# Repeated decay rows of a state-space mixer: from matmuls with ones to loads from DRAM, all four heads of a group at a time

## The reference

```
xbc = silu(causal_conv4(xbc));  xs, bm, cm = split(xbc)      # 4 groups of 4 heads, 64 wide; state 128
dt = softplus(dt_raw + dt_bias);  a_cum = cumsum(dt * -exp(a_log))       # per head and token
lmat = exp(where(l >= s, a_cum[l] - a_cum[s], -inf))
y_diag = (cm . bm) * lmat @ (xs * dt)
y_off = (cm . state_before) * exp(a_cum)
y = y_diag + y_off + d_skip * xs;  g = y * silu(z);  out = g * rsqrt(mean(g*g)) * norm_w
```

## Time and profile before

| what | value |
|---|---|
| median of 3 runs | 1801.18 us (1800.72 to 1802.22) |
| the profiled execution's own time | 1802.67 us |
| its span, first to last instruction | 1800.9 us |
| PE busy | 1749.4 us, 97% of the span |
| chain that ended last | PE 89%, DVE 7%, ACT 2% |
| DVE, ACT, POOL busy | 739.6, 636.9, 711.3 us |
| mean granted clock of TensorE | 0.99 |

### The profile page before, as it was taken

The page is one execution under the profiler, slowest core; times in us unless marked ns, Lnnn a source line. Parts: engine busy times, 40 slices in busy tenths (PEclk is TensorE's granted clock), DMA queues, the critical chain, the costliest instruction groups (busy, mean ns, idle before and its releaser), DMA issues.

```text
span 1800.9 us, 21799 instructions
## 1 busy us (share of the span) xinstructions
PE 1749.4 (97%) x7922; PEld 1413.6 (78%) x7922; DVE 739.6 (41%) x1230; ACT 636.9 (35%) x855; POOL 711.3 (39%) x303
## 2 busy tenths in 40 slices
PE   7999999999999999999899999999989999999996
PEld 6888888888888888888778777777748787888884
DVE  4222322222111324113653555537599544365226
ACT  5333332333222224213632545353352344352112
POOL 3433334334444444442344334333314333325445
PEclk9999999999999999999899999999999999999998
DMA  5432232232322334332433222122203222217322
GB/s 202 127 90 88 88 94 88 88 100 82 100 93 95 102 92 142 120 117 70 170 92 113 69 72 94 68 82 74 81 25 102 73 72 79 82 59 267 119 82 94
DMA packets 51260, 177.68 MB, mean 99 GB/s; under 512 B 5352, under 2 KB 5608, under 8 KB 50032
## 3 DMA queue, kind: packets, MB, share of 16 engines
q1 hardware_dynamic: 41472, 152.13, 26.9%
q10 hardware_dynamic: 9712, 24.48, 3.8%
HBM read 168.18 MB, written 8.40 MB: 98 GB/s over the span
## 4 chain that ended last, share of the span: by engine, by line
PE 89%; DVE 7%; ACT 2%; issue 1%; POOL 1%; DMA 0%; ACTq 0%; SPq 0%; DVEq 0%; POOLq 0%
PE bank L332 88%; PE bank L336 2%; DVE bias L1566 1%; DVE feats L1089 1%; DVE top L1562 1%; DVE bias L1089 1%; POOL w_lo L310 1%; ACT w_hi L718 0%; DMA raw<-in_stream 0%; DVE padded L1342 0%; ACT probsT L1018 0%; ACT bank L914 0%; ACT L1007 0%; DVE stats L1238 0%; DVE planes_lo L1285 0%
## 5 line engine op out<-in xcount | busy, mean ns | idle before, releaser
L310 POOL TENSOR_TENSOR w_lo<-raw,w_hi 128x1024 fp32r<-128x1024 f32 x280 | 685.7, 2453 | 1073.1 <-ACT w_hi L718 1073.1
L332 PE MATMUL bank<-planes_hi,w_hi 128*128 128x512 f32 (+1 forms) x1792 | 709.5, 396 | 19.1 <-DVE w_lo L1151 9.5
L332 PE MATMUL bank<-planes_lo,w_hi 128*128 128x512 f32 (+1 forms) x1792 | 694.7, 388 | 0.0
L332 PE MATMUL bank<-planes_hi,w_lo 128*128 128x512 f32 (+1 forms) x1776 | 687.7, 387 | 0.0
L718 ACT ACTIVATE w_hi<-raw 128x1024 fp32r<-128x1024 f32 x280 | 296.9, 1060 | 911.1 <-PE bank L332 876.9
L332 PEld LDWEIGHTS bank<-planes_hi,w_hi 128*128 128x128 f32 x1792 | 339.7, 190 | 104.0 <-issue 30.6
L332 PEld LDWEIGHTS bank<-planes_lo,w_hi 128*128 128x128 f32 x1792 | 340.1, 190 | 70.5 <-issue 4.8
L332 PEld LDWEIGHTS bank<-planes_hi,w_lo 128*128 128x128 f32 x1776 | 336.2, 189 | 68.1
L332 PE MATMUL bank<-w_hi,planes_hi 128*128 128x512 f32 x512 | 200.4, 391 | 0.0
L332 PE MATMUL bank<-w_hi,planes_lo 128*128 128x512 f32 x512 | 199.3, 389 | 0.0
L332 PE MATMUL bank<-w_lo,planes_hi 128*128 128x512 f32 x512 | 199.2, 389 | 0.0
(11 more groups left out here) (244 smaller groups left out, 1272.2 us busy)
## 6 DMA issues: line engine op xcount, KB each, us to landing
raw<-in_stream SPq DMA_DIRECT2D x282, 512.0 KB, 3.6
h_rows<-feats ACTq DMA_DIRECT2D x4, 1024.0 KB, 7.0
feats<-in_x_t SPq DMA_DIRECT2D x3, 1024.0 KB, 10.7
rope_q<-cum_dram ACTq DMA_DIRECT2D x8, 256.0 KB, 3.1
bias<-in_x_rows ACTq DMA_DIRECT2D x2, 1024.0 KB, 6.1
probs<-in_x_rows ACTq DMA_DIRECT2D x2, 1024.0 KB, 7.9
bias<-h_rows ACTq DMA_DIRECT2D x2, 1024.0 KB, 7.6
probs<-h_rows ACTq DMA_DIRECT2D x2, 1024.0 KB, 8.7
```

The source lines that it names most:

```text
L310: nc.gpsimd.tensor_sub(w_lo[:, s, :], raw[:, s, :], w_hi[:, s, :].bitcast(fp32)).then_inc(lo_ready, 1)
L332: return nc.tensor.matmul(o, a, b, start=start, stop=stop)
```

## The change

The rows are no longer repeated by PE. In the preparation ACT stores `cumT` and its exponential `R[2]` to a DRAM tensor `decay_dram`. For each group SP loads four rows of each, every row repeated over 128 partitions (256 KB a load): L rows into four `LB` tiles as soon as the heads of the group before are done, E rows into four `EB` tiles one weight unit later. These loads stand in SP's list between those of the weights. The tiles lie in buffers free at that time, for which the load of `rope_q` moves behind the stage and `R` from `probs` to `bias`.

All 16 spreads and 16 `pick_row` go, and so do the exponentials from PSUM. `segments` becomes a `tensor_scalar` in place in SBUF (subtract, minimum with zero); the mask is now a multiplication of the scores by zeros and ones, once per group, in PSUM. DVE makes the segments of all four heads in a row between `ssd_carry` and `conv_tile` 1. ACT takes their four exponentials in one go, after tile 1's `Silu`. `operands` 0 and 1 now stand behind `conv_tile` 2, operands 2 and 3 behind `conv_tile` 3; on PE the heads stay where they are.

```diff
+    decay_dram = nc.dram_tensor("decay_dram", [2 * SSD_HEADS, S], fp32, kind="Internal").ap()
...
-        LB = [tmp[:, :], probsT[:, 2, :]]
-        EB = [probsT[:, 3, :], qT[:, :]]
+        LB = [rope_q[:, 0, :], rope_q[:, 1, :], vN[:, 0, :, :].rearrange("p j n -> p (j n)"), gate[:, :]]
+        EB = [probsT[:, 3, :], qT[:, :], kT[:, 0, :], kT[:, 1, :]]
+        SQ = [tmp[:, :], probsT[:, 2, :]]
...
-        MM_STEPS, VEC_STEPS, EXP_STEPS = 14, 17, 10
+        MM_STEPS, VEC_STEPS, EXP_STEPS = 10, 13, 6
...
-            with sp.Fori(2, ROUNDS) as m:
+            def load_next(m, s):
+                sp.wait_ge(lo_ready, 4 * m + s - 7)
+                load(m, s)
+
+            def load_decay(g, of, bufs):
+                for r in range(4):
+                    row = SSD_HEADS * of + 4 * g + r
+                    sp.dma_start(bufs[r], decay_dram[row:row + 1, :].to_broadcast([P, S])).then_inc(decay_loaded[r], 16)
+
+            m0, p0 = tile_at(T_SSD, 6)
+            with sp.Fori(2, m0 + 2) as m:
                 for s in range(4):
-                    sp.wait_ge(lo_ready, 4 * m + s - 7)
-                    load(m, s)
+                    load_next(m, s)
+            for g in range(GROUPS):
+                for u in range(12):
+                    if u == 2 * p0:
+                        if g:
+                            sp.wait_ge(ssd_mm, MM_STEPS * (g - 1) + 9)
+                        else:
+                            sp.wait_ge(decay_kept, 32)
+                        load_decay(g, 0, LB)
+                    load_next(m0 + 2 + 3 * g + u // 4, u % 4)
+                    if u == 2 * p0:
+                        load_decay(g, 1, EB)
+            with sp.Fori(m0 + 2 + 3 * GROUPS, ROUNDS) as m:
+                for s in range(4):
+                    load_next(m, s)
...
-            step(nc.gpsimd.memset(upper[:, :], 0.0))
-
-            select(upper[:, :], ALU.is_ge, -BIG, 0, [[1, P]], -1)
+            step(nc.gpsimd.memset(upper[:, :], 1.0))
+
+            select(upper[:, :], ALU.is_ge, 0.0, 0, [[1, P]], -1)
...
-                srcs = [cumT[:, :]] + [probs[0:SSD_HEADS, k, :] for k in range(4)]
+                srcs = [cumT[:, :]] + [bias[0:SSD_HEADS, k, :] for k in range(4)]
...
-            def ssd_spread(g, r):
-                pe.wait_ge(ssd_vec, VEC_STEPS * g + (4, 6, 10, 13)[r])
-                mm([M, O][r % 2][:, :], ones[0:SSD_HEADS, :], gT[0:SSD_HEADS, :]).then_inc(ssd_mm, 1)
-
             def ssd_head(g, r):
-                pe.wait_ge(ssd_vec, VEC_STEPS * g + (10, 13, 15, 16)[r])
+                pe.wait_ge(ssd_vec, VEC_STEPS * g + 9 + r)
                 lanes = slice(64 * (r % 2), 64 * (r % 2) + 64)
-                dst, L, E = B[1 + r // 2], LB[r % 2], EB[r % 2]
+                dst, L, E = B[1 + r // 2], LB[r], EB[r]
...
                     ssd_states(g)
-                    ssd_spread(g, 0)
                 ssd_tile(6 * it + 2)
                 if g < 0:
                     spread_decay()
-                else:
-                    ssd_spread(g, 1)
                 ssd_tile(6 * it + 3)
                 if g >= 0:
                     ssd_head(g, 0)
-                    ssd_spread(g, 2)
                 ssd_tile(6 * it + 4)
                 if g >= 0:
                     ssd_head(g, 1)
-                    ssd_spread(g, 3)
                 ssd_tile(6 * it + 5)
                 if g >= 0:
...
-            act.dma_start(rope_q[:, :, :], rope_qk).then_inc(rope_q_loaded, 16)
...
             signal(nc.scalar.activation(R[2], cumT[:, :], ACT.Exp), prep_turn, 4)
+            act.dma_start(decay_dram[0:SSD_HEADS, :], cumT[:, :]).then_inc(decay_kept, 16)
+            act.dma_start(decay_dram[SSD_HEADS:2 * SSD_HEADS, :], R[2]).then_inc(decay_kept, 16)
...
             def ssd_exps(g, r):
-                act.wait_ge(ssd_vec, VEC_STEPS * g + (7, 9, 12, 14)[r])
-                n = EXP_STEPS * g + 2 * r + 1
-                signal(nc.scalar.activation(LB[r % 2], LB[r % 2], ACT.Exp), ssd_exp, n)
-                signal(nc.scalar.activation(EB[r % 2], [M, O][r % 2][:, :], ACT.Exp), ssd_exp, n + 1)
+                act.wait_ge(ssd_vec, VEC_STEPS * g + 5 + r)
+                signal(nc.scalar.activation(LB[r], LB[r], ACT.Exp), ssd_exp, EXP_STEPS * g + r + 1)
...
-                    if it and 1 <= k <= 4:
-                        ssd_exps(it - 1, k - 1)
+                    if it and k == 1:
+                        for r in range(4):
+                            ssd_exps(it - 1, r)
             t = tile_at(T_IDX, 6)
             turn_round(t)
+            act.dma_start(rope_q[:, :, :], rope_qk).then_inc(rope_q_loaded, 16)
...
-            def pick_row(g, r, value):
-                signal(V.tensor_scalar(gT[0:SSD_HEADS, :], cumT[:, :], ident[0:SSD_HEADS, at(4 * g + r)], None, MULT),
-                       ssd_vec, VEC_STEPS * g + value)
-
             def segments(g, r, value):
 
+                dve.wait_ge(decay_loaded[r], 32 * (g + 1))
                 for c in range(QB):
-                    chunk = slice(P * c, P * c + P)
-                    ins = stt(LB[r % 2][:, chunk], [M, O][r % 2][:, chunk], cumN[:, c, at(4 * g + r)], upper[:, :], SUB, ADD)
+                    cols = LB[r][:, P * c:P * c + P]
+                    ins = V.tensor_scalar(cols, cols, cumN[:, c, at(4 * g + r)], 0.0, SUB, MIN)
...
-                dve.wait_ge(ssd_exp, EXP_STEPS * g + 2 * r + 2)
-                L, E = LB[r % 2], EB[r % 2]
+                dve.wait_ge(ssd_exp, EXP_STEPS * g + r + 1)
+                L, E = LB[r], EB[r]
                 step(V.tensor_mul(L, L, B[0][:, :]))
                 signal(V.tensor_mul(E, E, XBC[g % 2][:, 1, :]), ssd_vec, VEC_STEPS * g + value)
...
-                    pick_row(g, 0, 4)
+                    scores = B[0][:, :].rearrange("p (c n) -> p c n", c=QB)
+                    step(V.tensor_mul(scores, scores, upper[:, :].unsqueeze(1).to_broadcast([P, QB, P])))
                 if it == 1:
                     dve.wait_ge(rows_stored, STORED[0])
                 conv_tile(6 * it)
                 if it >= 1:
                     ssd_carry(g)
-                    dve.wait_ge(ssd_mm, MM_STEPS * g + 6)
-                    pick_row(g, 1, 6)
-                    segments(g, 0, 7)
+                    for r in range(4):
+                        segments(g, r, 5 + r)
                 conv_tile(6 * it + 1)
-                if it >= 1:
-                    dve.wait_ge(ssd_mm, MM_STEPS * g + 7)
-                    pick_row(g, 2, 8)
-                    segments(g, 1, 9)
-                    operands(g, 0, 10)
                 if it == 1:
 
                     dve.wait_ge(rope_i_loaded, 16)
...
                 if it == 0:
                     take_decay()
                 if it >= 1:
-                    dve.wait_ge(ssd_mm, MM_STEPS * g + 9)
-                    pick_row(g, 3, 11)
-                    segments(g, 2, 12)
-                    operands(g, 1, 13)
+                    operands(g, 0, 9)
+                    operands(g, 1, 10)
                 conv_tile(6 * it + 3)
                 if it >= 1:
-                    dve.wait_ge(ssd_mm, MM_STEPS * g + 11)
-                    segments(g, 3, 14)
-                    operands(g, 2, 15)
-                    operands(g, 3, 16)
+                    operands(g, 2, 11)
+                    operands(g, 3, 12)
                 conv_tile(6 * it + 4)
```

More of the change, by code:

```diff
@@ L240, in block_kernel @@
         ln1_loaded = [sem(f"ln1_loaded{db}") for db in range(4)]
+        decay_kept, decay_loaded = sem("decay_kept"), [sem(f"decay_loaded{r}") for r in range(4)]
         prep_turn, prep_turned = sem("prep_turn"), sem("prep_turned")
@@ L581, in idx_scores @@
                         if t == 0 and SCORES[half][i - 1] is M:
-                            pe.wait_ge(ssd_exp, EXP_STEPS * (GROUPS - 1) + 9)
+                            pe.wait_ge(ssd_exp, EXP_STEPS * (GROUPS - 1) + 5)
                         mm(SCORES[half][i - 1][:, 0:n], QI[t][lanes, P * i:n], k_idx[lanes, 0:n]).then_inc(idx_scored, 1)
@@ L597, in ssd_turn @@
                     if src == 3 and g:
-                        pe.wait_ge(ssd_exp, EXP_STEPS * (g - 1) + 9)
+                        pe.wait_ge(ssd_exp, EXP_STEPS * (g - 1) + 5)
                     for c in range(QB):
@@ L626, in ssd_squares @@
             def ssd_squares(g):
-                pe.wait_ge(ssd_vec, VEC_STEPS * g + 17)
-                mm(M[:, :], ones[:, :], LB[0], True, False)
-                mm(M[:, :], ones[:, :], LB[1], False, True).then_inc(ssd_mm, 1)
+                pe.wait_ge(ssd_vec, VEC_STEPS * g + 13)
+                mm(M[:, :], ones[:, :], SQ[0], True, False)
+                mm(M[:, :], ones[:, :], SQ[1], False, True).then_inc(ssd_mm, 1)
             for it in range(GROUPS + 1):
@@ L958, in _ @@
             act.wait_ge(planes_ready, 48)
-            act.dma_start(rope_q[:, :, :], rope_qk).then_inc(rope_q_loaded, 16)
             turn_round(tile_at(T_MISC, 0))
             take(tile_at(T_MISC, 0), gT[:, :], T_MISC - SK + 1)
```

(22 more changed lines are left out.)

## The result

The changed kernel takes 1809.09 us (median of 6 runs, 1808.4 to 1810.03), against 1801.33 for the kernel before (6 runs in the same comparison): a ratio of 1.0042, with a 95% interval of 1.0032 to 1.0052. It is slower by 7.8 us, and 1809.0 was forecast.

The account below looks back on a forecast made before the run. PE, busy 97% of the span, was taken to bound the kernel. Spreads -17.5, stalls +4.6 and +14.6, clock +5.0 and stores +1.1 sum to +7.8 us: 1809.0 us forecast, range 1796 to 1816.

Parts of the forecast that it names:

- 16 spreads: PE's row-repeating products, four per group: removing them gains 1.04 us each for three and 1.26 for one, 17.5 us in all.
- waits at head 0: PE waits at each pass's first head for operands 0, now behind conv_tile 2: 4.6, 7.3, 7.3 and 0 us.
- clock behind them: After each of three PE stalls the clock falls to the 1.2 GHz level, 1.7 us each, 5.0 us in all.
- preparation: ACT's two stores ahead of tile 0's w_hi copies cost 1.1 us; moving the rope_q load was taken as nothing.
- Chain to head 0: Pass 2, from segments through conv_tile 1, ACT's take 2 and conv_tile 2 to operands 0: PE can start at 1095.2.
- standstill behind POOL: DVE stops for POOL's two units: segments lose 1.8 and 2.5 us in pass 2, and conv_tile 2 takes 5.5.
- two instructions of over 1 us: Sign expected in the profile after: conv_tile 2 holds two DVE instructions this long.
- Table switch: ACT's chain to take 2: the trace row adds nothing; the skill's drain adds 1.4 us in three passes, some 1813.
- (2): Rival: POOL doesn't stop DVE in the new order, pass 2 stalls only 0.4 us, time 1789.3 us; chance 0.17.
- (3): Rival: only POOL's first unit stops the segments and short stalls leave the clock, 1799.0 us; chance 0.13.
- (4): Rival: repeated rows land late among weight loads, delaying segments; 5 us too many give +15, 1824 us; chance 0.08.
- worst 0.3: Pass 4, head 0: no stall taken, since operands 0 end by 1253.3 and PE arrives at 1253.0; at worst 0.3 us.

Follow-up runs that it names:

- old-order run: The changed kernel's data path in the order of the kernel before, one exponential and one segment at a time: 1783.73 us, 0.9907.
- idle products: The changed kernel with 19 unused products ahead of head 0 in pass 1 and 28 each in passes 2 and 3: 1802.91 us, 1.0008.
- two runs that moved POOL's units: The changed kernel, ACT emptying tile 2's accumulator before its two w_hi copies in passes 1 to 3: 1807.63 us; those copies behind tile 2's Silu: 1798.18 us.
- run with late stores: The changed kernel's data path in the order of the kernel before, the two decay_dram stores moved behind tile 0's take and Silu: 1783.66 us.
- run with the copies behind `Silu` 2: The changed kernel, ACT emptying tile 2's accumulator first in passes 1 to 3, its two w_hi copies made behind tile 2's Silu: 1798.18 us, 0.9981.

## Why the prediction was right

The terms, as forecast and as the runs show them:

| term | forecast, us | measured, us | from |
|---|---|---|---|
| 16 spreads | -17.5 | -18.4 | timeline, old-order run |
| waits at head 0, passes 1, 2, 3, 4 | 4.6, 7.3, 7.3, 0 | 4.67, 6.75, 6.75, 0.42 | timeline after |
| clock behind them | 5.0 | 6.6 | products behind head 0; idle products: 6.2 |
| preparation | 1.1 | 0.5 | waits, two runs |
| sum | +7.8 | +7.3 | spans +6.8, medians +7.8 |

- **Spreads.** Spread 0 was priced like those behind a head, 1.04 us. Its neighbours are the products of `ssd_states`, and there the two timelines differ by 1.25: from the first of these products to the second product of the next tile are 2.77 us in the trace before and 1.52 in the trace after. That is 0.2 us more than priced in each of four passes.
- **Chain to head 0.** Its links in pass 2, forecast and measured: segments 9.4 and 8.9, `conv_tile` 1 2.95 and 2.9, ACT to the end of `take` 2 7.4 and 7.5, `conv_tile` 2 5.5 and 5.2 (6.85 and 2.92 in the two runs that moved POOL's units), operand 1.45 and 1.4. The standstill behind POOL was the uncertain part. It came as read from the pick and from `conv_tile` 3 of pass 1, in the segments and in `conv_tile` 2 of passes 2 and 3, and in `conv_tile` 2 alone in pass 1. Of the "two instructions of over 1 us" in `conv_tile` 2 one is (the three that take 4.28 us hold it), the other takes 0.92. By the Trainium skill (SBUF — State Buffer, Who interferes with whom) a DVE instruction with two SBUF inputs that comes second stands still until GpSimd's has ended. Both runs that move POOL's units agree: the three such steps of `conv_tile` 2 take 6.27 us with both units beside them and 2.33 with none.
- **Table switch.** The exponential begins at 1084.77, as soon as the load of 1083.47 has ended. The drain that the Trainium skill adds to a switch (ScalarE: Activation LUTs, What ACT_TABLE_LOAD costs) isn't seen. By that page's 1.38 us, once in each of three passes, the time would lie some 4 us above the measured one, an estimate.
- **Clock.** 3.4 us at half speed per wait was the row of before; it was 5.0, 3.3 and 5.7. A term of 5.0 measured 6.6. In that row the clock fell after PE had resumed; here it fell inside the waits, at about 1008.1, 1093.5 and 1178.8, and stayed down past their end. The two waits of 6.75 us lost 1.5 and 2.7 us, so the length of the wait alone does not give the price. What does, no run here isolates.
- **Preparation.** The issue of both stores took 0.93 us where 1.1 was forecast. The leaving of the `rope_q` load was taken as nothing and gave 0.4 back: from `take` of T_MISC to that of tile 0 are 17.74 us in the trace before and 17.32 in the run with late stores. DVE's first step of the preparation stands less long behind POOL, 2.0 us in place of 2.45. That this is the reason is read from the trace, not tested.
- **Rivals.** (2), no standstill, falls with the two runs that move POOL's units. (3), a single standstill and no fall of the clock, falls with the 6.29 us segments and the idle products. (4), late rows: a load takes 5.5 to 6.1 us to land where 3.1 was read the earlier trace rows, and the loads go out later than forecast (in pass 2 the L rows from 1041.9 and the E rows from 1050.5, not from 1038), but the last issue ends at 1052.4, 18.5 us before the first segment, and no wait in the stage names a DMA. In pass 4 the wait of 0.42 us is a little over the "worst 0.3" of the forecast.

That the sum came out within 0.1 us of the median is luck beyond this: the terms are off by -0.9, -0.6, +1.6 and -0.6, and single executions vary by 1 us.

## What to carry to other kernels

Taking work off the engine that sets the pace pays only if what feeds it keeps its place: a data path worth 17.5 us came out as 7.8 us more time, because one operand was put behind a step that needs two hand-overs between DVE and ACT, while four segments and four exponentials had made that step late. Either alone costs little: the late position 1.9 us of waiting, the batches nothing. Batching does harm when the first result of the batch is what the pacing engine wants next, so follow the first consumer's chain link by link, with the steps of other engines that the links stand still behind. And price a new wait of the pacing engine with the clock that it costs afterwards, here a third more on top.

## What the runs showed of the hardware

- Waits of 4.7 and 6.75 us were followed by 3.3 to 5.7 us at 1.2 GHz; after one of 0.97 us the clock stayed at 2.4 GHz. In the run with the copies behind `Silu` 2 it stayed up after a single wait of 2.42 us (pass 1), fell behind the second of two, 2.23 and 2.42 (pass 2), and fell inside one of 2.23 (pass 3, at about 1172.6). Products without use kept it up.
- Starting an SBUF step of DVE sooner can gain little if it then overlaps more with GpSimd: 2.2 us of head start turned into 0.6.
- A second copy of a matmul with `ones` costs 0.85 us, a single one between other shapes 1.04 to 1.26.
